# Down-projection of an encoder layer by seven block products for eight, the sums of features made by GpSimd beside the up-projection

## What is computed

```python
up, ffn_conv_state = causal_dwconv(x @ ffn_w_in, ffn_conv_prev, ffn_conv_w, ffn_conv_b)
gate, val = split_cols(up, (D_FF, D_FF))
x = layer_norm(DN_ALPHA * x + (jax.nn.silu(gate) * val) @ ffn_w_out, ln2_g, ln2_b)
```

## Time and profile before

| | |
|---|---|
| median of three executions | 2633.81 us (2633.74 to 2640.5) |
| the profiled execution | 2629.18 us |
| its span, first to last instruction | 2627.7 us |
| TensorE, VectorE, ScalarE, GpSimd busy | 96%, 62%, 41%, 7% of the span |
| mean granted clock of TensorE | 0.987 |
| `project_features` | from about 288 us to about 589 us |
| `ffn_up`, its matmuls | 1162 to 2108 us, the rounds begin at about 1162, 1509 and 1811 us |
| `ffn_down`, its matmuls | 2107.75 to 2617.5 us |

### The profile page before, as it was taken

One profiled execution on the slowest core, in us unless ns is written; L12 is line 12 of the kernel. 1 busy time (PEld: TensorE's weight loads), 2 busy tenths in 40 slices (PEclk: granted clock), 3 DMA queues, 4 the chain that ended last, 5 costly groups with the idle time before them and its releaser, 6 DMA issues. The chain is left out here.

```text
span 2627.7 us, 46682 instructions
## 1 busy us (share of the span) xinstructions
...
## 2 busy tenths in 40 slices
...
GB/s 205 147 141 213 146 128 152 83 106 181 121 131 129 265 136 184 206 161 278 240 252 238 259 291 260 260 258 230 256 257 257 227 197 114 82 80 92 84 77 62
DMA packets 406221, 472.11 MB, mean 180 GB/s; under 512 B 39387, under 2 KB 338941, under 8 KB 406099
## 3 DMA queue, kind: packets, MB, share of 16 engines
...
q10 hardware_dynamic: 998, 0.48, 0.1%
...
## 5 line engine op out<-in xcount | busy, mean ns | idle before, releaser
L2793 PE MATMUL fu_banks<-mo_fu_x_hi,mo_fu_w 128*128 128x354 f32 (+1 forms) x1848 | 605.6, 328 | 30.7 <-DVE fu_c L2756 9.8
L2795 PE MATMUL fu_banks<-mo_fu_x_hi,mo_fu_w 128*128 128x354 f32 (+1 forms) x1848 | 602.9, 326 | 0.0
L2794 PE MATMUL fu_banks<-fu_x_lo_rest,mo_fu_w 128*128 128x354 f32 (+1 forms) x1584 | 516.1, 326 | 0.0
L2793 PEld LDWEIGHTS fu_banks<-mo_fu_x_hi,mo_fu_w 128*128 128x128 f32 x1848 | 350.4, 190 | 40.9 <-DVE mo_fu_w L2665 10.1
L2795 PEld LDWEIGHTS fu_banks<-mo_fu_x_hi,mo_fu_w 128*128 128x128 f32 x1848 | 350.6, 190 | 0.0
L2794 PEld LDWEIGHTS fu_banks<-fu_x_lo_rest,mo_fu_w 128*128 128x128 f32 x1584 | 300.2, 190 | 0.0
L121 PE MATMUL fu_banks<-fu_fd_w,fu_fd_h_hi 128*128 128x512 f32 x704 | 275.3, 391 | 5.8 <-DVE fu_fd_h_lo L3017 5.8
L122 PE MATMUL fu_banks<-fu_fd_w,fu_fd_h_hi 128*128 128x512 f32 x704 | 274.4, 390 | 0.0
L123 PE MATMUL fu_banks<-fu_fd_w,fu_fd_h_lo 128*128 128x512 f32 x704 | 274.4, 390 | 0.0
L3017 DVE TENSOR_TENSOR fu_fd_h_lo<-fu_fd_h_raw,fu_fd_h_hi 128x256 fp32r<-128x256 f32 x174 | 73.4, 424 | 283.0 <-ACT fu_fd_h_hi L2980 282.8
L2980 ACT CAST fu_fd_h_hi<-fu_fd_h_raw 128x256 fp32r<-128x256 f32 (+1 forms) x185 | 73.7, 400 | 388.7 <-PE fu_banks L123 368.0
...
## 6 DMA issues: line engine op xcount, KB each, us to landing
mo_fu_w<-fu_w_split SPq DMA_DIRECT2D x176, 512.0 KB, 4.3
fu_w_raw<-ffn_w_in SPq DMA_DIRECT2D x131, 512.0 KB, 5.5
fu_w_split<-mo_fu_w SPq DMA_DIRECT2D x44, 1024.0 KB, 5.9
fu_fd_h_raw<-h_t SPq DMA_DIRECT2D x176, 128.0 KB, 2.1
h_t<-fu_val SPq DMA_DIRECT2D x88, 176.0 KB, 1.9
fu_fd_raw<-ffn_w_out SPq DMA_DIRECT2D x22, 512.0 KB, 4.7
x_rows<-pr_xr SPq DMA_DIRECT2D x16, 512.0 KB, 2.8
xt<-pr_xt SPq DMA_DIRECT2D x16, 512.0 KB, 4.0
```

What stands on the lines that cost most here:

```text
L2793: pe.matmul(out, wh, xh, start=first and k == 0, stop=False, skip_group_check=True)
L2794: pe.matmul(out, wh, xl, start=False, stop=False, skip_group_check=True)
L2795: last = pe.matmul(out, wl, xh, start=False, stop=k == KH - 1, skip_group_check=True)
```

## The change

The down-projection is cut into 2 x 2 blocks: rows into two halves of 1056 (the even and the odd blocks of 352 rows), features into even and odd tiles of 128 (11 each), columns into two halves of 512. The product of 2 x 2 blocks is then made by seven block products and sums for eight block products.

- The sums of the weight blocks (four matrices of 1408 x 512) are made by VectorE in `project_features`, 11 sets of four subtractions, each set behind a convolution in groups 1 to 5 (`fdw_at`, `sum_weights`), from 1 MB loaded by SyncE, and stored to `fd_w_sum`.
- The sums of the feature blocks are made by GpSimd in `ffn_up` (`half_sums`): behind an even unit one difference, behind an odd unit three sums. SyncE stores them (`store_sums`); per pair of units seven blocks are stored and not four. An even unit's second block lives in a buffer of its own. ScalarE, before it writes `val0`, `val1` or that buffer, now also waits for GpSimd (`sums_done`). In rounds two and three the half of the value weights that was not used is no longer loaded.
- `ffn_down` is new. It goes over 60 steps: the seven products one behind the other, each over eight row tiles (nine for four of them; the ninth holds the last 32 rows of both halves). A step is 33 matmuls of 512 columns into one bank. The features come in two pieces a step (6 and 5 tiles, 384 and 320 KB), ring of four. VectorE adds a finished bank into one to three places of the 16 results in SBUF (`take`), splits the next product's weights, and makes the norms: the first half's tiles during the fifth and sixth product, the second half's during the seventh. Nothing in it is a loop; every step is written out.
- In the last unit of `ffn_up` now all weights of the first product and the features of two steps are loaded, and TensorE issues 33 matmuls ahead.

The core of the diff:

```diff
+FD_ORDER, FD_NINE = (1, 2, 3, 5, 6, 7, 4), (1, 2, 3, 5)
...
+        def fdw_at(g, p, i, j):
+            if isinstance(g, int):
+                return {1: 0, 3: 1, 5: 2}.get(j) if g == 1 else None
+            if p:
+                return 4 * i + 2 if j == 0 else None
+            return {1: 4 * i - 1, 3: 4 * i, 5: 4 * i + 1}.get(j)
...
+                def sums_of(kk):
+                    sp.wait_ge(fdw_done, 4 * kk + 4)
+                    alone(sp)
+                    pair = slice(kk, kk + 1) if isinstance(kk, int) else bass.ds(kk, 1)
+                    sp.dma_start(d["fd_w_sum"][pair].rearrange("a p c -> p (a c)"), fdw_sum[:].rearrange("p s c -> p (s c)")).then_inc(fdw_stored, 16)
+                sp.wait_ge(w_lo_done, KD - 1)
+                load_fdw(0)
 
...
+                        kk = fdw_at(g, p, i, j)
+                        if kk is not None:
+                            sums_of(kk)
+                            if not (p if not isinstance(g, int) else kk == 2):
+                                load_fdw(kk + 1)
+                        if not isinstance(g, int) and p == 0 and j == 0:
+                            load_fdw(4 * i - 1)
...
+                pool.wait_ge(fdw_stored, 16 * (KF // 2))
...
+                    b11, b12, b21, b22 = (fdw_raw[:, e, c:c + 512] for e in range(2) for c in (0, 512))
+                    dve.wait_ge(fdw_loaded, 16 * kk + 16)
+                    wait_if(dve, fdw_stored, 16 * kk)
+                    alone(dve)
+                    dve.tensor_tensor(fdw_sum[:, 0], b12, b11, ALU.subtract).then_inc(fdw_done, 1)
+                    dve.tensor_tensor(fdw_sum[:, 2], b22, b12, ALU.subtract).then_inc(fdw_done, 1)
+                    dve.wait_ge(fdw_done, 4 * kk + 1)
+                    alone(dve)
+                    dve.tensor_tensor(fdw_sum[:, 1], b22, fdw_sum[:, 0], ALU.subtract).then_inc(fdw_done, 1)
+                    dve.wait_ge(fdw_done, 4 * kk + 3)
+                    alone(dve)
+                    dve.tensor_tensor(fdw_sum[:, 3], fdw_sum[:, 1], b21, ALU.subtract).then_inc(fdw_done, 1)
...
+                def store_sums(q, j, p):
+                    u = KF * q + j
+                    n = width(q)
+                    cols = slice(352 * q, 352 * q + n)
+                    sp.wait_ge(sums_done, 2 * u + 1 + p)
+                    alone(sp)
+                    if p:
+                        sp.dma_start(h_sum[:, :, one_tile(j), cols].rearrange("p s a c -> p (s a) c"), half_sum[:, :, :n]).then_inc(sums_stored, 16)
+                    else:
+                        sp.dma_start(flat(h_mix[:, one_tile(j), cols]), evens(q, j)[1][:, :n]).then_inc(diff_stored, 16)
...
+                        sp.wait_ge(mm_done, 7 * (NU - 1))
+                        sp.wait_ge(h_stored[0], 16 * KF)
+                        for n in range(4):
+                            ks = slice(*FD_PIECES[n % 2])
+                            first = h_val.rearrange("p (k e) c -> e p k c", e=2)[0]
+                            sp.dma_start(fd_h_raw[:, n, 0:ks.stop - ks.start, :],
+                                         first[:, ks, n // 2 * P:(n // 2 + 1) * P]).then_inc(fd["h_loaded"][n], 16)
                     for i in range(7):
...
+                def half_sums(q, j, p):
+                    u = KF * q + j
+                    n = width(q)
+                    even, diff = evens(q, j)
+                    if p == 0:
+                        wait_if(pool, diff_stored, 8 * u)
+                        pool.wait_ge(h_done, 2 * u + 2)
+                        alone(pool)
+                        pool.tensor_tensor(diff[:, :n], val0[:, :n], even[:, :n], ALU.subtract).then_inc(sums_done, 1)
+                        return
+                    s1, s2, s4 = (half_sum[:, i, :n] for i in range(3))
+                    wait_if(pool, sums_stored, 8 * u - 8)
+                    pool.wait_ge(h_done, 2 * u + 2)
+                    pool.wait_ge(sums_done, 2 * u - 1)
+                    alone(pool)
+                    pool.tensor_tensor(s1, even[:, :n], val1[:, :n], ALU.add).then_inc(sums_done, 1)
+                    pool.tensor_tensor(s2, val1[:, :n], diff[:, :n], ALU.subtract).then_inc(sums_done, 1)
+                    pool.wait_ge(sums_done, 2 * u + 1)
+                    alone(pool)
+                    pool.tensor_tensor(s4, val0[:, :n], s2, ALU.subtract).then_inc(sums_done, 1)
...
+                    wait_if(act, sums_done, 2 * u - p)
...
+                for n, (k0, k1) in enumerate(FD_PIECES):
+                    pe.wait_ge(fd["h_lo_done"], n + 1)
+                    for k in range(k0, k1):
+                        if k % 2 == 0:
+                            pe.wait_ge(fd["w_lo_done"], k // 2 + 1)
+                        high, low, _ = fd_w_piece(k // 2)
+                        last = products(pe, banks[:, 3], fd_h_hi[:, n, k - k0], fd_h_a[:, n, k - k0], high[:, k % 2], low[:, k % 2],
+                                        k == 0, k == KF // 2 - 1)
                     last.then_inc(fd["piece_done"], 1)
...
+        steps = [(i, which, t) for i, which in enumerate(FD_ORDER) for t in range(9 if which in FD_NINE else 8)]
...
+        operand = {1: even(h_val), 2: odd(h_val), 3: odd(h_sum[:, 2]), 4: odd(h_mix), 5: odd(h_sum[:, 0]), 6: odd(h_sum[:, 1]), 7: even(h_mix)}
+        weight_sum, weight_block = {5: 0, 6: 1, 7: 2, 4: 3}, {1: (0, 0), 2: (1, 0), 3: (1, 1)}
...
+                def load_h(n):
+                    _, which, t = steps[n // 2]
+                    k0, k1 = FD_PIECES[n % 2]
+                    sp.wait_ge(piece_done, n - 3)
+                    for src, col, at, cols in sources(which, t):
+                        sp.dma_start(h_raw[:, n % RING, 0:k1 - k0, at:at + cols], src[:, k0:k1, col:col + cols]).then_inc(h_loaded[n % RING], 16)
...
+                    elif which == 3:
+                        add((0, t, 1), p)
+                        dve.wait_ge(x_loaded[t % 2], x_count(8 + t))
+                        add_residual((1, t, 1), 8 + t, None, (1, t, 0))
+                        add_residual((1, t, 0), 8 + t, None, (1, t, 0))
+                    elif which == 5:
+                        add((0, t, 1), p)
+                        add((1, t, 1), p)
+                        statistics((0, t), 0)
+                    elif which == 6:
+                        add((0, t, 1), p)
+                        add((1, t, 0), p)
+                        add((1, t, 1), p)
+                    elif which == 7:
+                        add((1, t, 0), p)
+                        add((1, t, 1), p)
+                        statistics((1, t), 1)
+                    else:
+                        add((1, t, 0), p, ALU.subtract)
+                    assert counts["added"] == n_added[s]
...
+                for s in range(1, NS):
+                    if s + 1 < NS:
+                        lo(2 * s + 2)
+                    take(s - 1)
+                    for order, item in enumerate(norms):
+                        if end_of.get(item) == s:
+                            finish(order)
+                    if prepares(s) is not None:
+                        split_w(steps[s][0] + 1, prepares(s))
+                    if s + 1 < NS:
+                        lo(2 * s + 3)
+                    for order, item in enumerate(norms):
+                        if begin_at[item] == s:
+                            begin(order)
+                            if item[0]:
+                                finish(order)
+                take(NS - 1)
+                begin(16)
...
+                def step(s):
+                    i, which, t = steps[s]
+                    out = bank(s)
+                    await_bank(pe, ("step", s))
+                    for piece, (k0, k1) in enumerate(FD_PIECES):
+                        n = 2 * s + piece
+                        pe.wait_ge(h_lo_done, n + 1)
+                        for k in range(k0, k1):
+                            if t == 0 and k % 2 == 0:
+                                pe.wait_ge(w_lo_done, 6 * i + k // 2 + 1)
+                            w_hi, w_lo = (w_piece(i, k // 2, e)[:, k % 2, :] for e in range(2))
+                            high, low = h_hi[:, n % RING, k - k0], h_a[:, n % RING, k - k0]
+                            if t == NINTH:
+                                pe.matmul(out, high, w_hi, start=k == 0, stop=False)
+                                last = pe.matmul(out, high, w_lo, start=False, stop=k == KK - 1)
+                            else:
```

727 lines of the change are left out of this document (438 added, 289 removed).

## The result

The changed kernel took 2648.4 us (median of 7 runs, 2641.7 to 2653.0), the kernel before 2633.8 us (7 runs, 2631.1 to 2640.5): a ratio of 1.0048, 95% interval 1.0034 to 1.0063, 0.5% slower. The prediction said 2596 us, 1.4% faster. The profiled run of the changed kernel took 2649.2 us with a span of 2647.7 us.

The account below looks back on a forecast made before the run. It took VectorE to bound the up-projection's first round and TensorE the rest. 2629.2 - 60 - 6 - 1 + 16 + 13 = 2591 us, with 4.6 us to the median 2596 us; own range 2578 to 2612, wider range 2564 to 2622.

Parts of the forecast that it names:

- Term 5: Feature projection: VectorE's sums of weights and their late loads stall TensorE, 13 us more, ends 0 and 22.
- Nothing waits for the sums themselves: Feature projection: GpSimd's load of the bias, queued behind the weight sums, is covered by 82 us of idle time.
- the walk through groups 1 and 2: Feature projection: added sums delay VectorE, stalling TensorE 3 and 5 us, then up to 8 us; 8 to 16 together.
- VectorE in the down-projection: Down-projection: VectorE's work averages 7.3 us a step at its fullest against TensorE's 7.46, so costed at nothing.
- rounds two and three unchanged to 3 us: Up-projection: predicted sign that the second and third rounds keep their time to 3 us; longer would prove the prediction wrong.
- Term 4: Up-projection, first round: GpSimd's sums hold up VectorE operations with two SBUF inputs, 16 us more, ends 0 and 33.
- Term 1: Down-projection: 265 fewer matmuls at 0.226 us each, 60 us less.
- I am wrong if the matmul rate falls below one in 0.24 us: Down-projection: sign that would refute the prediction, matmuls coming slower than one in 0.24 us in the last stage.
- Term 2: Hand-over from up-projection to down-projection: 4 us of stall instead of 10, 6 us less, between 10 less and 5 more.
- VectorE becomes the bound: Down-projection rival: waits in VectorE's chain add 0.6 us to each of 24 norm steps, 14 us, 2610 us; chance 0.13.
- Term 3: End of the kernel: VectorE adds 512 columns, takes one statistic, and the final store is in two parts, 1 us less.
- a lock in all three rounds: Up-projection rival: each of GpSimd's 132 operations delays TensorE by 0.76 us, 100 instead of 16 us, 2680 us; chance 0.05.

Follow-up runs that it names:

- e1: Changed kernel with ten of the eleven sets of weight sums made of 8 columns instead of 512, loads and stores kept: span 2618.0 us.
- e11: Changed kernel with a second tile for the loaded weights, so each load for the weight sums is issued one set earlier: span 2627.6 us.
- e2: Changed kernel with GpSimd's feature sums 8 columns wide instead of 352 in the 18 middle units of each round: span 2629.6 us.
- e3: Changed kernel with first down-projection weight loads issued a unit earlier in round three and feature sums stored before split weights in round one: span 2630.0 us.
- e5: Changed kernel with three SBUF addresses moved so all down-projection feature and weight tiles start at offset 128 within 512 bytes: span 2634.5 us.
- e6: Changed kernel with the first eight weight tiles of every second product swapped in place with the first half of the results: span 2641.7 us.
- e9: Changed kernel with down-projection features at offset 384 within 512 bytes, three weight tiles at 128 and the fourth at 384: span 2633.9 us.

## Why the prediction was wrong

On the scale of the profiled run the sum was 2591 us and the run took 2649.2, 58 more: 23 in term 5, 16 in the down-projection, 12 in round three, 9 in the second stretch with its clock, and 2.6 less in the rest.

- **Term 5** (sums of weights, 13 us more, ends 0 and 22) is the step that failed first: 36 us, outside its own ends. Two sentences of it were wrong. The first is "Nothing waits for the sums themselves": GpSimd waited 95 us for their last store, its load of the bias went out 132 us later than before, and an idle time of 82 us did not cover that; it and the loads behind it met the stores of the last group, 10.1 us there and 1.7 behind it. The other is the size of the walk through groups 1 and 2. It was of the right kind and named the right products: TensorE did wait before products 4 and 8 of group 2, for 6.4 and 3.7 us where the walk had 3 and 5. But groups 2 to 4 lost 24 us for its 8 to 16, part of it at the low clock, which the walk left out. e1 and e11 show that neither the waits nor the subtractions alone, but their sum in an ordered queue, ran over the slack.
- **A wait that I did not see.** "VectorE in the down-projection" and "the hand-over" were walked, "with the loads and splits for 33 more" was written, but not where those splits stand. Two orders that contradict each other (SyncE's load behind its wait for a product, ScalarE's split ahead of what the product after it needs) cost 12 us in round three, in a round that I had priced at 0 because VectorE is idle for a third of it. A share of idle time does not cover a wait that stands in front of the product's own release. The sentence "rounds two and three unchanged to 3 us" was the test for it, and it came out wrong in round three.
- **Term 4** (GpSimd beside round one, 16 us more) had the mechanism right and its size too high: 10 us by e2. The predicted delays behind an odd unit were 0.4, 0.7 and 0.8 us less 0.5 (which is 1.4, not 1.5); the earlier trace rows against the rows above give 0.7, 0.7 and 0.3, and since a unit grew by 1.06 us, 0.6 of it went into idle time: about 1 us a pair instead of 1.5. The Trainium skill, "SBUF — State Buffer", section "Who interferes with whom", has the lock for VectorE instructions with two inputs in SBUF and not for one in PSUM, and the rows agree (0.68 to 1.36 us; 0.52 unchanged). Another 5 us of round one were the store order at the turn (e3), which no term had.
- **Term 1** (265 matmuls at 0.226, 60 us less) was right for what is left out: 264 and 59.9 (1940 matmuls and not 1938; the four with the identity stayed four). But it took the pitch of the old stage for the new one. 11 us were given back, because features and weights start at different offsets within 256 bytes (e5, e6, e9). "I am wrong if the matmul rate falls below one in 0.24 us" was too coarse a test for this.
- **Term 2** (hand-over, 6 us less) came out as 2.6: the wait behind the matmuls issued ahead is 2.7 us from start to start for 5.3, and the low clock behind it stayed (eight starts at about 0.4 us, six before). All stalls of the stage together are only 1.2 us less, since 3 us of new ones stand further on, 1.4 and 1.6 where TensorE waits for VectorE's low parts. These are a small piece of the rival *VectorE becomes the bound*, which was priced at 14.
- **Term 3** (the end, 1 us less): 0.7.
- **The rivals.** None was it. The slower side was a lock in all three rounds; rounds two and three show next to none of it (e2 changes each by 0.5 us at most). The chance of 0.05 for slower came from having looked for one mechanism only. Four places in the order of queues were worth 24, 12, 12 and 5 us: the late loads and sums, GpSimd's wait for their stores, the load in round three and the store at the turn. The forecast's own range was also added up a little low: half the ends of terms 2, 4 and 5 give 2580 to 2615 us, not 2578 to 2612.
